# First norm's squares added on GpSimd, one product with ones in the middle of the second unit, and an output projection that waits tile by tile

## Chip, cores and metric

The kernel runs on one core of one Trainium2 chip. The metric is the device time of one execution in microseconds (us), lower is better; several executions are summed up by their median. In the text PE is the TensorE matrix engine, DVE the VectorE, ACT the ScalarE, POOL the GpSimd and SP the SyncE (it issues DMAs only).

## The reference

One decoder layer for 576 tokens (512 of a prompt, 64 of eight decode sequences), width 1024, feed-forward width 2816, all in float32:

```python
def rmsnorm(x, g):
    y = xf * lax.rsqrt(jnp.mean(xf * xf, axis=-1, keepdims=True) + RMS_EPS)
    return (y * g).astype(x.dtype)

def half_swiglu(x, g, w_gate, w_up, w_down):
    h = rmsnorm(x, g)
    return x + 0.5 * ((jax.nn.silu(h @ w_gate) * (h @ w_up)) @ w_down)

x = half_swiglu(x, ffn1...)                       # first feed-forward half step
proj = rmsnorm(x, mix_norm) @ w_in                # attention q/k/v, RWKV rows, gates
o_attn = ...dilated window attention...           # three groups of heads
o_rwkv = ...RWKV-7 time mixing...
merged = sigmoid(g_attn) * (o_attn @ w_branch_attn) + sigmoid(g_rwkv) * (o_rwkv @ w_branch_rwkv)
x = x + merged @ w_out                            # output projection
x = half_swiglu(x, ffn2...)                       # second feed-forward half step
```

Outputs are the new x, the key and value caches, the RWKV state and the token-shift rows.

## The kernel before

**Layout.** Everything is kept transposed: a tensor of width 1024 is 8 tiles (KD = 8) of 128 partitions by 576 tokens. A matmul covers 288 tokens, so each tile takes two.

**Three passes.** Float32 accuracy is had from splits: an operand is its high part (written by ACT as fp32r) plus its low part (value minus high part, by DVE for activations, by POOL for weights). One *slice* (`unit_slice`, L343) is the six matmuls of one input tile: high by high, low by high, high by low, twice 288 columns. One *unit* is the slices that make one tile of 128 output columns: 8 slices for weights of 1024 rows (`W8`, 128x1024 elements). Units come in pairs P with two sides q = 0 and 1, each side with its own `w_raw`, `w_hi`, `w_lo` and PSUM banks (side 0 writes banks 0 and 1, side 1 banks 2 and 3, banks 4 and 5 take the norm's sums). There are 101 pairs.

**The flow of a unit's weights.** SP loads `w_raw` (L319) once POOL has finished the pair before; ACT copies it to `w_hi` (`split_hi`, L325) once PE has finished with the old one; POOL subtracts to `w_lo` (`split_lo`, L330); PE waits for that (`unit_wait`) and for its PSUM banks to be read.

**The first norm.** `first_act` and `first_dve` go over the 8 tiles of x. DVE multiplies a tile by the gain (`h_gained`, L464), ACT copies the product to `h_hi` (`h_high`, L455), DVE subtracts to `h_lo` (`h_low`, L460). ACT also squares each tile (`square`, L421) into one of two buffers, and PE adds the squares over partitions by a float32 product with a matrix of ones (`sum_squares`, L428), one product for each of the 8 tiles, each put ahead of that tile's slice of the very first unit. A third square waits until PE has read the first one. The weights are split after the second and the fourth tile. After the last product the root follows: Ln and Exp on ACT (L367, L368), a refinement on DVE (L375, L376, L379) that ends in `nry`. DVE multiplies `nry` into the first unit's result (L596), ACT applies Silu to it (L560), and only after that, in ACT's own order, splits the weights of the next pair.

**The middle and the second norm.** The norm ahead of w_in and the one ahead of the second feed-forward step add their squares on DVE (`add_square`, L402) and need one product with ones (`sum_all`, L408).

**Merge and output projection.** `merge_pe` runs four units of the attention branch in halves, whose results DVE reads from PSUM bank pairs, multiplies by a gate (L2131) and adds to the RWKV half (L2135). ACT writes `m_hi` (L2108), DVE `m_lo` (L2121), which counts `m_ready` up by one for each of the 8 merged tiles, from 1. The output projection is pairs P_OUT to P_OUT+3; PE starts it when `m_ready` is 8, that is with seven tiles, and waits for the eighth before its slice. DVE adds each unit to x (L2144).

Every engine runs its instructions in the written order, and waits only on semaphores.

## Time and profile before

| | |
|---|---|
| median of 3 runs | 1896.87 us |
| lowest, highest | 1893.55, 1899.52 us |
| the profiled execution | 1897.97 us |
| its span, first to last instruction | 1896.1 us |
| PE busy | 1791.2 us, 94% of the span |
| DVE, ACT, POOL busy | 41%, 32%, 28% |
| mean granted TensorE clock | 0.973 of full |

The profile is one execution recorded by the hardware. Its rows give a start and a length in us from the span's start; the bracket behind a row is how long the engine had been idle and what ended the wait. A clock of 1.00 is 2.4 GHz and 0.50 is 1.2 GHz. Times below are span times; the execution's own time is 1.9 us more than its span.

### The profile page before, as it was taken

The page shows a single profiled execution, that of the slowest core. Times are in us where ns is not written, and L with a number is a line of the kernel's source. Part 1 is how long each engine was busy: PE and PEld are TensorE (multiplying, and loading weights), DVE is VectorE, ACT ScalarE, POOL GpSimd, SP SyncE. Part 2 cuts the span into 40 slices and gives each one's busy share as a digit, 9 for nine tenths or more (in the row PEclk, how much of TensorE's full clock was granted, in tenths as well). Part 3 has the DMA queues.
Part 4 walks back from the last instruction along what each step waited for, and adds up shares of the span by engine and source line. Part 5 has one row for each costly group of instructions (what it writes and reads, how often), then busy time and mean ns, then how long its engine had stood idle before and what let it go on. Part 6 is the DMA issues. An engine that isn't in the chain of part 4 may idle for free.

```text
span 1896.1 us, 41228 instructions
## 1 busy us (share of the span) xinstructions
PE 1791.2 (94%) x17032; PEld 1700.9 (90%) x17032; DVE 769.4 (41%) x1111; ACT 610.0 (32%) x806; POOL 537.3 (28%) x210
## 2 busy tenths in 40 slices
PE   6999999997989898989979999999989999999999
PEld 6999999996989898988758989898889999999999
DVE  4333023323564545552367272727367333113320
ACT  4332122222524242422134253435223333123321
POOL 2333333332312121211012222223223343433432
PEclk9999999998999999999789999999989999999999
DMA  4333233331533232321034444535443333334343
GB/s 159 111 122 130 103 111 129 130 123 51 187 127 105 79 134 106 112 70 48 34 126 167 160 161 145 194 131 188 167 188 127 106 112 132 127 100 133 111 142 123
DMA packets 53111, 237.49 MB, mean 125 GB/s; under 512 B 7040, under 2 KB 7680, under 8 KB 51584
## 3 DMA queue, kind: packets, MB, share of 16 engines
q1 hardware_dynamic: 45120, 219.40, 33.6%
q10 hardware_dynamic: 7872, 16.37, 2.3%
q8 instruction: 91, 1.49, 0.3%
q14 instruction: 28, 0.23, 0.0%
HBM read 217.98 MB, written 71.76 MB: 153 GB/s over the span
## 4 chain that ended last, share of the span: by engine, by line
PE 55%; issue 24%; DVE 11%; POOL 5%; ACT 2%; DVEq 1%; ACTq 1%; POOLq 0%; PEldq 0%; PEld 0%
PE ps L343 41%; POOL w_lo L330 5%; PE ps L785 3%; DVE qkv L1932 2%; DVE work L375 1%; DVE work L376 1%; PE ps L1791 1%; DVE qkv L1089 1%; PE ps L1729 1%; DVEq L1983 1%; PE ps L1715 1%; ACT w_hi L325 1%; DVE probs L379 0%; DVE xx L1130 0%; PE ps L1329 0%
## 5 line engine op out<-in xcount | busy, mean ns | idle before, releaser
L330 POOL TENSOR_TENSOR w_lo<-w_raw,w_hi 128x1024 fp32r<-128x1024 f32 (+1 forms) x202 | 531.5, 2631 | 1339.6 <-ACT w_hi L325 1339.6
L343 PE MATMUL ps<-h_hi,w_hi 128*128 128x288 f32 x2464 | 556.1, 308 | 23.9 <-DVE h_lo L460 10.7
L343 PE MATMUL ps<-h_lo,w_hi 128*128 128x288 f32 x2464 | 531.3, 298 | 0.0
L343 PE MATMUL ps<-h_hi,w_lo 128*128 128x288 f32 x2464 | 531.2, 297 | 0.0
L343 PEld LDWEIGHTS ps<-h_hi,w_hi 128*128 128x128 f32 x2464 | 401.6, 191 | 48.8 <-issue 19.7
L343 PEld LDWEIGHTS ps<-h_lo,w_hi 128*128 128x128 f32 x2464 | 401.4, 191 | 0.0
L343 PEld LDWEIGHTS ps<-h_hi,w_lo 128*128 128x128 f32 x2464 | 400.8, 191 | 0.0
L325 ACT ACTIVATE w_hi<-w_raw 128x1024 fp32r<-128x1024 f32 (+1 forms) x204 | 226.3, 1109 | 460.2 <-PE ps L343 442.9
L343 PE MATMUL ps<-g_hi,w_hi 128*128 128x288 f32 x704 | 151.4, 297 | 0.1
L343 PE MATMUL ps<-g_lo,w_hi 128*128 128x288 f32 x704 | 151.2, 296 | 0.0
L343 PE MATMUL ps<-g_hi,w_lo 128*128 128x288 f32 x704 | 151.0, 296 | 0.0
L599 DVE SCALAR_TENSOR_TENSOR gt<-ps,nry 128x576 f32<-128x576 f32 x44 | 33.4, 758 | 241.3 <-PE ps L343 241.3
L612 DVE SCALAR_TENSOR_TENSOR x<-ps,x 128x576 f32 (+1 forms) x32 | 24.2, 758 | 236.0 <-PE ps L343 236.0
L343 PEld LDWEIGHTS ps<-g_hi,w_hi 128*128 128x128 f32 x704 | 113.6, 188 | 1.1 <-POOL w_lo L330 1.1
L343 PEld LDWEIGHTS ps<-g_lo,w_hi 128*128 128x128 f32 x704 | 113.7, 189 | 0.0
L343 PEld LDWEIGHTS ps<-g_hi,w_lo 128*128 128x128 f32 x704 | 113.7, 188 | 0.0
L605 DVE TENSOR_TENSOR g_lo<-gt,g_hi 128x576 f32 x44 | 87.6, 1990 | 42.2 <-ACT g_hi L565 42.2
L560 ACT ACTIVATE sg<-sg 128x576 f32<-128x576 f32 x44 | 30.2, 687 | 161.0 <-DVE sg L596 161.0
L596 DVE SCALAR_TENSOR_TENSOR sg<-ps,nry 128x576 f32<-128x576 f32 x44 | 33.4, 758 | 91.1 <-PE ps L343 90.6
L1352 ACT ACTIVATE qkv<-ps 128x576 f32<-128x576 f32 x36 | 23.4, 651 | 137.8 <-PE ps L343 137.7
L1013 ACT ACTIVATE zz<-ps 128x256 f32<-128x256 f32 x40 | 15.4, 384 | 90.5 <-PE ps L785 89.3
L560 ACT ACT_TABLE_LOAD x30 | 38.5, 1283 | 13.2 <-issue 13.2
(369 smaller groups left out, 1962.5 us busy)
## 6 DMA issues: line engine op xcount, KB each, us to landing
w_raw<-in_w SPq DMA_DIRECT2D x172, 512.0 KB, 3.7
w_raw<-in_w SPq DMA_DIRECT2D x32, 704.0 KB, 4.0
kv<-in_kc SPq DMA_DIRECT2D x32, 576.0 KB, 6.5
kv<-in_vc SPq DMA_DIRECT2D x32, 576.0 KB, 7.7
cache_out<-in_cache SPq DMA_DIRECT2D x28, 576.0 KB
gates<-gate_out ACTq DMA_DIRECT2D x16, 288.0 KB, 2.3
cache_out<-in_cache SPq DMA_DIRECT2D x8, 480.0 KB
kvT<-qkv ACTq DMA_DIRECT2D x4, 864.0 KB, 7.8
```

The source lines that it names most:

```text
L325: nc.scalar.activation(w_hi[par_][:, 0:words], w_raw[par_][:, 0:words], ACT.Copy).then_inc(hi_done, 1)
L330: nc.gpsimd.tensor_tensor(w_lo[par_][:, 0:words], w_raw[par_][:, 0:words], w_hi[par_][:, 0:words].bitcast(F32), ALU.subtract).then_inc(lo_ ...
L343: last = nc.tensor.matmul(ps[:, b + c, 0:HC], w[par_][:, wk], a[:, k, c * HC:(c + 1) * HC], start=(first and k == 0), stop=(end and k == n ...
L375: own(nc.vector.tensor_tensor(rt, ry, ry, ALU.mult))
L560: nc.scalar.activation(sg[:, :], sg[:, :], ACT.Silu).then_inc(sem("silu_done"), 1)
L596: nc.vector.scalar_tensor_tensor(two(sg[:, :]), bank2(0), back(0), two(nry[:, :]), ALU.mult, ALU.mult).then_inc(evac[0], 1)
L599: nc.vector.scalar_tensor_tensor(two(gt[:, :]), bank2(2), back(0), two(nry[:, :]), ALU.mult, ALU.mult).then_inc(evac[1], 1)
L605: nc.vector.tensor_tensor(g_lo[:, j, :], gt[:, :], g_hi[:, j, :].bitcast(F32), ALU.subtract).then_inc(sem("g_ready"), 1)
L612: nc.vector.scalar_tensor_tensor(two(x[:, k, :]), bank2(2 * q), 0.5, two(x[:, k, :]), ALU.mult, ALU.add)\
L785: last = nc.tensor.matmul(ps[rows_of(e), 4 + (2 * n + h) % 4, 64 * T:64 * T + 64], lhs(T, e), rhs(T, e), start=True, stop=True)
L1352: nc.scalar.activation(two(QKV[:, g, kind, :]), bank2(bank), ACT.Copy).then_inc(evac[q], 1)
L1932: V.scalar_tensor_tensor(a, a, P1("qg" if kind == 0 else "kg", g), ary[i % 2], ALU.mult, ALU.mult)\
```

## The change

Four edits at the start of the kernel and one at the output projection:

- The first norm's squares are added up in `nrt_first` by POOL (`add_first`), seven additions of 128x576: three after the split of the first weights, four after the split of the second. ACT writes the first square straight into `nrt_first`; its square k from k = 3 on waits for addition k-2.
- PE makes one product with ones, `sum_all(pe, 0)`, between slices 3 and 4 of the second unit, in place of eight in the first unit.
- ACT splits the first weights after the first square, ahead of the first `h_high` (before: after the second tile).
- The parameters follow the first two tiles of x in ACT's DMA queue; the first part of the constants goes behind all of x. ACT's first square now waits for the parameters too.
- The first unit pair of the output projection is written out of its loop: unit 0 waits for merged tile k ahead of slice k.

```diff
-        ACC = (None, nrt_first, mA)
+        ACC = (nrt_first, nrt_first, mA)
...
-            pe.wait_ge(sem("sq_added"), 7 * m)
+            pe.wait_ge(sem("sq_added"), 7 * m + 7)
...
-            if m:
-                if k == 0:
-                    out = ACC[m]
-                elif k >= 3:
-                    act.wait_ge(sem("sq_added"), 7 * (m - 1) + k - 2)
-            elif k >= 2:
-                act.wait_ge(sem("sq_summed"), k - 1)
+            if k == 0:
+                out = ACC[m]
+            elif k >= 3:
+                act.wait_ge(sem("sq_added"), 7 * m + k - 2)
...
                 if k % 2 == 0:
-                    act.wait_ge(sem("x_loaded%d" % (k // 2)), 16)
+                    act.wait_ge(sem("x_loaded%d" % (k // 2)), 16 if k else 32)
                 square(act, 0, k, k % 2)
+                if k == 0:
+                    split_hi(act, 0, 0, W8)
                 h_high(act, 0, k, k % 2)
-                if k in (1, 3):
-                    split_hi(act, 0, k // 2, W8)
+                if k == 3:
+                    split_hi(act, 0, 1, W8)
...
-            if f == 0:
-                pe.wait_ge(sem("con_loaded"), 32)
-                sum_squares(pe, 0, 0, 0, start=True)
             unit_wait(pe, P0, 0)
             for k in range(KD):
-                if f == 0 and k:
-                    sum_squares(pe, 0, k, k % 2, stop=(k == KD - 1))
...
-            unit(pe, P0, 1)
+            unit_wait(pe, P0, 1)
+            for k in range(KD):
+                if f == 0 and k == KD // 2:
+                    pe.wait_ge(sem("con_loaded"), 16)
+                    sum_all(pe, 0)
+                last = unit_slice(1, h_hi, h_lo, k, k, KD, 2)
+            last.then_inc(unit_done, 1)
...
+        def add_first(pool, k):
+            pool.wait_ge(sem("sq_ready"), k + 1)
+            nc.gpsimd.tensor_tensor(ACC[0][:, :], ACC[0][:, :], SQ[0][k % 2][:, :], ALU.add).then_inc(sem("sq_added"), 1)
+            pool.drain()
...
+            split_lo(pool, P0, 0, W8)
+            if P0 == P_FFN1:
+                for k in range(1, 4):
+                    add_first(pool, k)
+            split_lo(pool, P0, 1, W8)
+            if P0 == P_FFN1:
+                for k in range(4, KD):
+                    add_first(pool, k)
...
-            pe.wait_ge(sem("m_ready"), KD)
-            units_and_squares(pe, 2, P_OUT, lambda P, q: unit(pe, P, q, m_hi, m_lo, ready=("m_ready", 1, KD - 1)))
+            unit(pe, P_OUT, 0, m_hi, m_lo, ready=("m_ready", 1, 0))
+            unit(pe, P_OUT, 1, m_hi, m_lo)
+            with pe.Fori(1, 4) as j:
+                for q in range(2):
+                    unit(pe, P_OUT + j, q, m_hi, m_lo)
...
-                    act.dma_start(con[:, 0:CFIRST], t["con"][:, 0:CFIRST]).then_inc(sem("con_loaded"), 16)
-                    act.dma_start(par[:, :, 0], t["par"]).then_inc(sem("con_loaded"), 16)
+                    act.dma_start(par[:, :, 0], t["par"]).then_inc(sem("x_loaded0"), 16)
+            act.dma_start(con[:, 0:CFIRST], t["con"][:, 0:CFIRST]).then_inc(sem("con_loaded"), 16)
```

How this moves instructions. ACT at the start, before (rows of the program's order: line, operation, output from inputs, size, what it waits for):

```order
L421 ACTIVATE sq<-x 128x576 [waits x_loaded0]
L455 ACTIVATE h_hi<-hf_first 128x576 [waits hf_ready]
L421 ACTIVATE sq<-x 128x576
L455 ACTIVATE h_hi<-hf_first 128x576 [waits hf_ready]
L325 ACTIVATE w_hi<-w_raw 128x1024 [waits w_loaded_even]
L421 ACTIVATE sq<-x 128x576 [waits sq_summed,x_loaded1]
```

and after (lines have shifted; L418 is the square, L444 the high part):

```order
L418 ACTIVATE nrt_first<-x 128x576 [waits x_loaded0]
L325 ACTIVATE w_hi<-w_raw 128x1024 [waits w_loaded_even]
L444 ACTIVATE h_hi<-hf_first 128x576 [waits hf_ready]
L418 ACTIVATE sq<-x 128x576
L444 ACTIVATE h_hi<-hf_first 128x576 [waits hf_ready]
L418 ACTIVATE sq<-x 128x576 [waits x_loaded1]
```

The split of the first weights stands one square and two high parts earlier, and the third square waits for PE no more.

POOL at the start has nothing but the two splits before; after, with the additions as L632:

```order
L330 TENSOR_TENSOR w_lo<-w_raw,w_hi 128x1024 [waits hi_done]
L632 TENSOR_TENSOR nrt_first<-nrt_first,sq 128x576 [waits sq_ready] x3
L330 TENSOR_TENSOR w_lo<-w_raw,w_hi 128x1024 [waits hi_done]
L632 TENSOR_TENSOR nrt_first<-nrt_first,sq 128x576 [waits sq_ready] x4
L637 UNCONDITIONAL_BRANCH
```

So POOL has nine instructions in the stretch in which DVE makes `h_lo`, where it had two.

PE in the middle of the second unit, after; before, these slices followed each other with no product between:

```order
L343 MATMUL ps<-h_hi,w_hi 128x288 x2
L343 MATMUL ps<-h_lo,w_hi 128x288 x2
L343 MATMUL ps<-h_hi,w_lo 128x288 x2
L408 MATMUL ps<-nrt_first,con 128x288 [waits sq_added,con_loaded]
L408 MATMUL ps<-nrt_first,con 128x288
L343 MATMUL ps<-h_hi,w_hi 128x288 x2
L343 MATMUL ps<-h_lo,w_hi 128x288 x2
```

Twelve slices stand ahead of the one product with ones; seven stood ahead of the last of the eight.

## Rows read from the trace of the kernel before

**Rows 1.** The page: busy time of each engine, share of the span, instructions

```profile
PE 1791.2 (94%) x17032; PEld 1700.9 (90%) x17032; DVE 769.4 (41%) x1111; ACT 610.0 (32%) x806; POOL 537.3 (28%) x210
```

**Rows 2.** DMAs: size, issue to landing; timeline of the first rows: start, length, instruction

```profile
con<-in_con ACTq DMA_DIRECT2D x1, 192.0 KB, 6.4
...
1.25 0.45 ACTq L2194 DMA_DIRECT2D con<-in_con  x1
...
6.66 0.68 ACT L421 ACTIVATE sq<-x 128x576 f32<-128x576 f32 x1 [0.65 <-DMA x<-in_xT]
8.85 1.14 DVE L464 TENSOR_SCALAR hf_first<-x,par 128x576 f32<-128x576 f32 x2 [8.85 <-DMA par<-in_par]
```

**Rows 3.** Timeline: first weights' split, first slice, ACT's longest wait, two later matmul pairs

```profile
11.70 1.06 ACT L325 ACTIVATE w_hi<-w_raw 128x1024 fp32r<-128x1024 f32 x1
12.83 2.40 POOL L330 TENSOR_TENSOR w_lo<-w_raw,w_hi 128x1024 fp32r<-128x1024 f32 x1 [12.38 <-ACT w_hi L325]
15.28 0.85 PE L343 MATMUL ps<-h_hi,w_hi 128*128 128x288 f32 x2 [4.13 <-POOL w_lo L330]
19.04 0.68 ACT L421 ACTIVATE sq<-x 128x576 f32<-128x576 f32 x1 [4.70 <-PE ps L428]
19.29 0.68 PE L343 MATMUL ps<-h_lo,w_hi 128*128 128x288 f32 x2
21.48 0.42 PE L343 MATMUL ps<-h_lo,w_hi 128*128 128x288 f32 x2
```

**Rows 4.** Timeline: last low part, last product, next pair, and the units behind it

```profile
28.37 0.76 DVE L460 TENSOR_TENSOR h_lo<-hf_first,h_hi 128x576 fp32r<-128x576 f32 x1 [0.68 <-ACT h_hi L455]
29.25 1.13 PE L428 MATMUL ps<-sq,con 128*128 128x288 f32 x4
37.49 5.20 POOL L330 TENSOR_TENSOR w_lo<-w_raw,w_hi 128x1024 fp32r<-128x1024 f32 x2 [13.34 <-ACT w_hi L325]
38.52 1.93 DVE L602 TENSOR_TENSOR gt<-sg,gt 128x576 f32<-128x576 f32 x1 [0.16 <-issue]
39.89 0.53 PE L343 MATMUL ps<-h_hi,w_hi 128*128 128x288 f32 x2 [2.32 <-POOL w_lo L330]
48.09 0.76 DVE L596 SCALAR_TENSOR_TENSOR sg<-ps,nry 128x576 f32<-128x576 f32 x1 [4.79 <-PE ps L343]
60.89 0.76 DVE L596 SCALAR_TENSOR_TENSOR sg<-ps,nry 128x576 f32<-128x576 f32 x1 [1.85 <-PE ps L343]
```

**Rows 5.** One POOL and one DVE instruction in the middle; the line's x4: shortest, median, longest ns

```profile
506.95 2.54 POOL L330 TENSOR_TENSOR w_lo<-w_raw,w_hi 128x1024 fp32r<-128x1024 f32 x1 [3.87 <-ACT w_hi L325]
...
507.33 2.48 DVE L1077 TENSOR_SCALAR qkv<-u_k,par 128x576 f32<-128x576 f32 x1
...
L1077 DVE TENSOR_SCALAR qkv<-u_k,par x4: 520/522/2483, 507.3 to 784.7; 128x576 f32<-128x576 f32 x4
L2250 POOL TENSOR_TENSOR rw_lo<-o_rw,rw_hi x4: 1421/1440/1457, 1319.5 to 1323.6; 128x576 fp32r<-128x576 f32 x4
```

**Rows 6.** Timeline of the merge: DVE's low parts, POOL's split, the output projection's first units

```profile
1404.33 0.76 DVE L2121 TENSOR_TENSOR m_lo<-sig_r,m_hi 128x576 fp32r<-128x576 f32 x1
...
1406.95 2.72 DVE L2121 TENSOR_TENSOR m_lo<-mrg,m_hi 128x576 fp32r<-128x576 f32 x1
1409.77 0.76 DVE L2121 TENSOR_TENSOR m_lo<-sig_r,m_hi 128x576 fp32r<-128x576 f32 x1
1418.06 0.76 DVE L2144 TENSOR_TENSOR x<-x,ps 128x576 f32<-128x576 f32 x1 [7.53 <-PE ps L343]
...
1406.23 2.83 POOL L330 TENSOR_TENSOR w_lo<-w_raw,w_hi 128x1024 fp32r<-128x1024 f32 x1 [5.20 <-ACT w_hi L325]
...
1410.07 0.82 PE L343 MATMUL ps<-m_hi,w_hi 128*128 128x288 f32 x2 [7.80 <-DVE m_lo L2121]
```

**Rows 7.** Stretches: length, busy time of each engine, PEclk the granted clock, DMA

```profile
1410.00:1412.80 2.80, 2.73 (x11) 2.77 (x12) 0.52 (x1) 0.00 (x0) 0.00 (x0) 0.50 1.01 375
...
40.70:43.90 3.20, 3.20 (x15) 3.20 (x15) 1.88 (x1) 1.85 (x2) 1.99 (x1) 0.50 0.59 173
```

More of the change, by code:

```diff
@@ L413, in square @@
             out = SQ[m][q]
-            if m:
-                if k == 0:
-                    out = ACC[m]
-                elif k >= 3:
-                    act.wait_ge(sem("sq_added"), 7 * (m - 1) + k - 2)
-            elif k >= 2:
-                act.wait_ge(sem("sq_summed"), k - 1)
+            if k == 0:
+                out = ACC[m]
+            elif k >= 3:
+                act.wait_ge(sem("sq_added"), 7 * m + k - 2)
             nc.scalar.activation(out[:, :], x[:, k, :], ACT.Square).then_inc(sem("sq_ready"), 1)
             act.drain()
-        def sum_squares(pe, m, k, q, start=False, stop=False):
-            pe.wait_ge(sem("sq_ready"), 8 * m + k + 1)
-            for c in range(2):
-                last = nc.tensor.matmul(ps[:, 4 + c, 0:HC], K("ones"), SQ[m][q][:, c * HC:(c + 1) * HC], start=start, stop=stop)
-            last.then_inc(sem("sq_summed"), 1)
         def units_and_squares(pe, m, P0, one):
@@ L435, in units_and_squares @@
                 one(P0 + j, 1)
-            if m == 1:
-                sum_all(pe, 1)
+            sum_all(pe, m)
         def splits_and_squares(act, m, P0, words):
@@ L637, in ffn_dve, with up, down @@
                     added(P0 + 15 + HALF + k // 2, k, k % 2, last=True)
+        def add_first(pool, k):
+            pool.wait_ge(sem("sq_ready"), k + 1)
+            nc.gpsimd.tensor_tensor(ACC[0][:, :], ACC[0][:, :], SQ[0][k % 2][:, :], ALU.add).then_inc(sem("sq_added"), 1)
+            pool.drain()
         def ffn_pool(pool, P0):
-            with pool.Fori(0, 2) as half:
-                with pool.Fori(0, HALF) as j:
+            def up(half, j0):
+                with pool.Fori(j0, HALF) as j:
                     for q in range(2):
                         split_lo(pool, P0 + 15 * half + j, q, W8)
+            def down(half):
                 with pool.Fori(0, 4) as j:
```

7 lines of the change are left out of this document (5 added, 2 removed).

## The prediction

> **What bounds the kernel now.** I read the page's busy times first: PE works 94% of the span [rows 1], and no other engine half of it. So the time is PE's work plus the places where PE stands still or runs at the low clock, and a change that takes little work from PE can gain only there. The timeline then gives the two places that this change touches. At the start PE idles until the first weights are split, works through the first unit with a product with ones ahead of each slice, and after the second unit waits again until 39.89 for the next pair's low weights [rows 3, 4]. From there on PE doesn't stop: two units take 60.89 - 48.09 = 12.80 us [rows 4], so one takes 6.40 and a slice 0.80. So the start is worth exactly what moves the 39.89. At the merge PE idles 7.80 us until the seventh merged tile is there [rows 6]. Between the two places the change touches nothing but code layout, so both shifts are carried to the end.
>
> **The start: what sets 39.89.** It is not PE's own work. The last product with ones ends at 29.25 + 1.13 = 30.38, and 9.51 us after that the next pair's first matmul starts [rows 4]; in between stand the root, multiplication into the first result, Silu, split, low part, each behind the one before. This chain is unchanged. The question is when the (now single) product ends.
>
> **Start, step 1: earlier weights.** The constants landed 1.25 + 6.4 = 7.65, the parameters at 8.85 [rows 2]. Without the constants ahead, the parameters come between 6.6 (the first x was used at 6.66) and 8.85; I take 7.8, which is 1.2 us behind their forerunner, as in the trace. The square then ends at 8.5, the split (1.06) at 9.7, POOL's low part (2.40) at 12.1, where it ended at 15.23 before [rows 3]. That is 3.1 us earlier. ACT's waits for PE vanish too, 4.70 us the longest [rows 3], and PE's eight products (1.13 each, [rows 4]) become one. But by step 2 DVE now sets the pace of this unit, so what both leave free goes into waiting for DVE.
>
> **Start, step 2: POOL and DVE block each other.** This is what the addition on POOL costs. While POOL subtracts, a DVE instruction on two SBUF tiles does not run: `m_lo` came at 1406.95, inside POOL's 1406.23 to 1409.06, and ended 0.61 after POOL (2.72 in place of 0.76) [rows 6]. A multiplication by a column, the form of `h_gained`, waits too: at 507.33, inside POOL's 506.95 to 509.49, it took 2.48 in place of 0.52, and ended 0.32 after POOL [rows 5]. The other way round, two low parts of 2.40 in a row took 5.20 with a DVE instruction between them, and the second ended 2.24 after that DVE instruction [rows 4]: POOL gets on about 0.15 before DVE's recorded end, and the two take turns. An addition is not in the trace; the nearest row is POOL's subtraction of the same size, 1.44 [rows 5], which I take (1.35 to 1.7 for the range, since a drain follows each).
>
> Here the Trainium skill speaks against this change: "SBUF — State Buffer", section "Who interferes with whom", says that GpSimd and a VectorE instruction with two SBUF inputs or in a 2-port mode lock each other out for a whole instruction, and that one with a single SBUF input outside these modes doesn't. Read so that `h_gained` (one input tile) is free, the sum would be that of the first rival below; the 2.48 us row says that it isn't.
>
> Nine POOL instructions (two splits, seven additions) now stand among DVE's sixteen. Stepping them through with these numbers, ACT at 0.69 for a square or high part: low part 0 comes at 10.5 in POOL's split and ends at 12.7 (first slice 12.8, before 15.28 [rows 3]); addition 1 to 14.0, `h_gained` 2 held to 14.3; addition 2 to 15.6, low part 1 held to 16.2; addition 3 to 17.5, `h_gained` 3 to 17.8; low parts 2 and 3 free, 18.7 and 20.1; split 1 to 22.4, `h_gained` 5 held to 22.7; addition 4 to 23.9, low part 4 to 24.6; addition 5 to 25.8, `h_gained` 6 to 26.1; addition 6 to 27.4, low part 5 to 28.1; addition 7 to 29.3, `h_gained` 7 to 29.6; low parts 6 and 7 at 30.5 and 31.3. Before, the last low part ended at 29.13 [rows 4]. So the 3.1 us of step 1 are gone before the last tile, and 2.2 more.
>
> **Start, step 3: the product stands later.** It waits for twelve slices in PE's order. Slices 6 and 7 of the first unit start at 30.5 and after it, then come four of the second unit, then the product (1.13, [rows 4]). A slice is 0.80 at 2.4 GHz and 1.44 at 1.2 GHz (six times 288 columns). PE stands still between slices up to then (eight slices over 19 us), so I take it to be at the low clock at 30.5. In two places where it went on without a stop it was at 0.50 for 2.8 and 3.2 us [rows 7]; in the first unit of the program it was still slow 4.0 us after its start at 15.28 (0.68 for two matmuls at 19.29) and fast at 21.48 (0.42), so after 4.7 to 6.2 us [rows 3]. I take 4.2 us, the middle: slices 6 and 7 end at 33.4, the next at 34.8, three fast ones at 37.2, the product at 38.3. All fast would be 36.5, all slow 41.1.
>
> **Start, sum.** 38.3 + 9.5 = 47.8 for the next pair's first matmul, against 39.89: **8.0 us later** (all fast 6.1, 6.2 us slow 8.8, all slow 10.7). The second unit is done by 42, so it is not late, and PE idles some 6 us in place of 2.3. Leaving PE at the low clock afterwards is paid in both: 39.89 to 48.05 is 8.16 for a unit of 6.40 [rows 4].
>
> **The output projection.** PE ended the attention branch at 1410.07 - 7.80 = 1402.27 [rows 6]. Merged tiles 5, 6 and 7 are ready at 1405.09, 1409.67 and 1410.53 [rows 6], the ones before earlier. The first unit's low weights were done by 1406.23 - 5.20 = 1401.03, when POOL fell idle [rows 6], and DVE had read its banks, which the tiles before 6 came from. So slices 0 to 5 run at once (6 x 0.80, to 1407.1, tile 5 in time), slice 6 from 1409.7, slice 7 from 1410.6 to 1411.4. Before, the first unit ended at 1418.0, when DVE read it [rows 6]: 6.6 us earlier. The next side's weights are ready at 1406.23 + 2.83 = 1409.06 [rows 6], in time. Against it stands the clock. Before, the 7.80 us cost 2.8 us at 0.50 after the restart [rows 7], within the 7.95 us of the first unit. Now PE idles 2.6 us; after 2.32 us of idleness at 39.89 the clock also fell, for 3.2 us [rows 4, 7]. So I take it to fall again: 1.6 us, as 3.2 us at half rate. The gain is **5.0 us** (4.6 to 6.9: a longer low stretch, or none and 0.3 us of the loop's entry saved, since 1410.07 is 0.4 after tile 6). DVE's own chain of the merge doesn't change, and the chain behind the projection moves with PE's units. The loop entered one pair later, and POOL's and PE's longer code, have no row; I take 0, with 0.5 either way.
>
> **Sum.** 8.0 - 5.0 = +3.0 us: span 1899.1, execution 1897.97 + 3.0 = 1901.0. The profiled execution is 1.1 above the median of the runs, so the median becomes 1896.87 + 3.0 = **1899.9 us**, 0.16% more. A measurement of this kernel can tell about 0.3%, 5.7 us, from no change: under 1891.2 is faster, over 1902.6 slower. Each part is larger than the difference.
>
> **Rivals.**
> - *DVE isn't held where it matters* (0.17). If `h_gained` ran beside POOL, the same stepping ends the last low part at 27.0 and, with PE's clock as above, starts the next pair at about 43.5; with nothing held, it ends at 24.2 (POOL's additions at 24.8), the product at 29.4 to 31.3, and the next pair starts at 38.9 to 40.8. So the start costs -1.0 to 3.6 and the projection gains 5.0: -6.0 to -1.4 together, median 1890.9 to 1895.5. For it: low parts 2 and 3 are free in my own stepping, so a shift in phase frees more. Against: no row of POOL at work shows such a DVE instruction at its normal length.
> - *PE stays at the low clock until the product* (0.15). This is the slower side: six slices and the product take the all-slow price, 41.1 + 9.5 = 50.6, 10.7 us late; less 5.0 that is +5.7, or 1902.6, and with the 4.6 or additions of 1.7 us it is 1904 to 1905. It decides from where the clock comes back 8 us or more after slice 6; the long slow stretch of the first unit before, 4.7 us or more, speaks for it [rows 3], the two stretches of 2.8 and 3.2 against [rows 7].
> - *The first unit isn't the brake at all* (0.06): POOL and DVE interleave and the clock is up early, so that the product ends near 29; the start gains 1, the projection 6.6, together 1889. The two rows of held DVE instructions speak against it.
> - *The tile-by-tile waits don't start the projection early* (0.05), because its weights or banks come late: the gain of 5 goes, and the median is 1904.9. The 1401.03 speaks against it.
> - The forecast has the remaining 0.57.
>
> **How the numbers follow.** The forecast's own range is 1897 to 1903: start 6.1 to 9.5, projection 4.6 to 6.9, and runs of the same kernel spread by 3 us either way. The range over the cases is 1891.5 to 1904.5: it takes in most of the first two rivals and leaves about 0.1 out on each side. Faster by over 0.3%: 0.12 (the third rival, and a third of the first with the runs' spread). Slower: 0.20 (the second rival mostly, the fourth, the tail of the forecast). Within: 0.68.
>
> **What would show it.** In the changed kernel's timeline: the first slice near 12.8; POOL's additions at about 1.45 alone and 1.9 when they follow a held DVE instruction; `h_gained` and low parts at 1.5 to 2.5 in place of 0.52 and 0.76; the last low part near 31; the product ending near 38 and the first matmul of the next pair near 48. In the merge: six slices right behind the attention branch, a gap of 2.6, the first unit read 6 to 7 us earlier after its own shift, a low clock behind the gap. Wrong would be: DVE instructions at normal length inside POOL's additions, a product before 34, or a projection that starts no earlier.

## The result

The changed kernel takes 1904.18 us (median of 13 executions, 1899.02 to 1914.7), the kernel before 1898.02 us (13 executions beside it): ratio 1.004, 95% interval 1.0026 to 1.0054. So it is slower by some 6 to 8 us. The prediction set 0.3% as what can be told; the middle of the interval lies above that, its lower end just below. The forecast was +3.0 us. Three further groups of executions of the changed kernel gave 1.0052, 1.0047 and 1.0046.

The page of the changed kernel's profile (1906.01 us, span 1904.2) gives PE the same busy time as [rows 1] within 1 us, and 7 us more for DVE and 12 for POOL. The second row is one of its DMA queues: packets, MB, share of the 16 engines. 1.51 MB in 92 packets is 16.4 KB each (16,384 bytes in the trace). The profile calls this queue "instruction"; I read its packets as pages of the engines' code, which matter below.

```profile
PE 1792.1 (94%) x17004; PEld 1703.0 (89%) x17004; DVE 776.3 (41%) x1111; ACT 610.1 (32%) x806; POOL 549.5 (29%) x217
...
q8 instruction: 92, 1.51, 0.3%
```

**The start** in the changed kernel's timeline (start, length, engine, line, instruction, idle time ahead and what ended it). It answers to [rows 2 to 4]; L343 and L330 keep their lines, `h_gained` is now L453, `h_low` L449, the addition L632, the product L408.

```profile
7.54 0.68 ACT L418 ACTIVATE nrt_first<-x 128x576 f32<-128x576 f32 x1 [1.90 <-DMA par<-in_par]
...
9.45 2.35 POOL L330 TENSOR_TENSOR w_lo<-w_raw,w_hi 128x1024 fp32r<-128x1024 f32 x1 [9.00 <-ACT w_hi L325]
...
11.76 1.93 POOL L632 TENSOR_TENSOR nrt_first<-nrt_first,sq 128x576 f32<-128x576 f32 x1
12.50 1.49 DVE L453 TENSOR_SCALAR hf_first<-x,par 128x576 f32<-128x576 f32 x1
...
12.55 0.82 PE L343 MATMUL ps<-h_hi,w_hi 128*128 128x288 f32 x2 [12.55 <-DVE h_lo L449]
...
13.84 1.42 POOL L632 TENSOR_TENSOR nrt_first<-nrt_first,sq 128x576 f32<-128x576 f32 x1 [0.16 <-issue]
...
19.88 2.46 DVE L453 TENSOR_SCALAR hf_first<-x,par 128x576 f32<-128x576 f32 x1
...
29.37 1.61 DVE L449 TENSOR_TENSOR h_lo<-hf_first,h_hi 128x576 fp32r<-128x576 f32 x2
...
37.35 1.13 PE L408 MATMUL ps<-nrt_first,con 128*128 128x288 f32 x4
...
47.98 0.85 PE L343 MATMUL ps<-h_hi,w_hi 128*128 128x288 f32 x2 [6.31 <-POOL w_lo L330]
```

Everything is where the prediction put it, and the next pair starts 8.1 us later than the 39.89 of [rows 4].

**The merge** of the changed kernel, which answers to [rows 6, 7]; the last row is a stretch (length, busy time of PE, PEld, DVE, ACT, POOL, granted clock, DMA share, GB/s).

```profile
1417.24 0.43 PE L343 MATMUL ps<-m_hi,w_hi 128*128 128x288 f32 x2
...
1424.53 0.84 PE L343 MATMUL ps<-m_hi,w_hi 128*128 128x288 f32 x2 [2.33 <-DVE m_lo L2135]
...
1427.88 0.76 DVE L2158 TENSOR_TENSOR x<-x,ps 128x576 f32<-128x576 f32 x1 [2.55 <-PE ps L343]
...
1424.50:1427.90 3.40, 3.37 (x14) 3.37 (x15) 0.78 (x2) 0.03 (x1) 0.00 (x0) 0.51 0.91 308
```

PE had ended the attention branch at 1417.40. The projection's first matmuls stand right behind it, PE waits 2.33 us for the seventh tile, and runs at half the clock (0.51, the level of 1.2 GHz) behind it. The first result is read at 1427.88 against 1418.06: 9.8 us later, where PE ended the attention branch 15.1 us later (1417.40 against 1402.27). So the projection gave back 5.3 us there.

It gave back 1.5 us more further on. In the kernel before, PE waits 2.33 us at 1480.40 for the first weights of the second feed-forward step and falls to the low clock; in the changed kernel it waits as long and doesn't (first two rows before, then two after, then the two stretches of 4.20 us behind the wait):

```profile
1480.40 0.53 PE L343 MATMUL ps<-h_hi,w_hi 128*128 128x288 f32 x2 [2.33 <-POOL w_lo L330]
...
1481.89 0.69 PE L343 MATMUL ps<-h_lo,w_hi 128*128 128x288 f32 x2
...
1490.36 0.53 PE L343 MATMUL ps<-h_hi,w_hi 128*128 128x288 f32 x2 [2.33 <-POOL w_lo L330]
...
1491.52 0.42 PE L343 MATMUL ps<-h_lo,w_hi 128*128 128x288 f32 x2
...
1480.40:1484.60 4.20, 4.20 (x20) 4.20 (x21) 2.44 (x2) 1.97 (x2) 2.80 (x1) 0.59 0.48 141
...
1490.36:1494.56 4.20, 4.20 (x31) 4.20 (x32) 2.47 (x2) 1.97 (x2) 2.82 (x1) 1.00 0.47 139
```

This isn't the chance of one profile: of the 12 profiles below with the projection by tiles 11 have no low clock there (after_r3 has), and all 8 without it have. No run shows why. So from the end of the attention branch to 1500 us the edit of the projection is worth 6.3 to 6.8 us in those 11.

**What was not forecast** lies between. I matched PE's instructions one by one in both traces. The stretch from 440.10 to 1400.10 of the kernel before holds no edited line, and the same 10,349 matmuls take 6.6 us longer in the changed kernel. First the kernel before, then the changed one (same columns as above):

```profile
440.10:1400.10 960.00, 885.72 (x10349) 800.85 (x10348) 491.63 (x836) 330.40 (x512) 191.31 (x79) 0.95 0.36 130
```

```profile
448.65:1415.24 966.59, 890.60 (x10350) 805.70 (x10349) 492.12 (x837) 331.07 (x513) 191.21 (x79) 0.95 0.36 129
```

PE is busy for 4.9 us more with the same work, which is the low clock, and stands still for 1.7 us more (966.59 - 890.60 = 75.99 against 74.28). The bill of the two profiles: start +8.1, up to 440 us +0.5, the untouched stretch +6.6, projection -5.3, behind it -1.8 (the 1.5 of the low clock that is missing at 1481 us, and 0.3 in small pieces), together +8.1, as the spans say. The question for the experiments is the 6.6.

### The profile page after: what moved, and what is told of

Same layout as the page of the kernel before. It is cut to its first block, busy times and chain, and to the rows that moved or that the text cites. A ratio compares the mean times of both kernels' runs of the same rounds, so it can differ in the third digit from the quotient of the medians.

```text
span 1904.2 us, 41116 instructions
## 1 busy us (share of the span) xinstructions
PE 1792.1 (94%) x17004; PEld 1703.0 (89%) x17004; DVE 776.3 (41%) x1111; ACT 610.1 (32%) x806; POOL 549.5 (29%) x217
## 3 DMA queue, kind: packets, MB, share of 16 engines
q8 instruction: 92, 1.51, 0.3%
## 4 chain that ended last, share of the span: by engine, by line
PE 60%; issue 17%; DVE 13%; POOL 4%; ACT 3%; DVEq 1%; ACTq 1%; POOLq 1%; DMA 0%; PEldq 0%; PEld 0%
PE ps L343 45%; POOL w_lo L330 4%; PE ps L796 3%; DVE qkv L1943 2%; PE ps L1802 1%; DVE work L375 1%; DVE work L376 1%; PE ps L1740 1%; DVE m_lo L2135 1%; PE ps L1726 1%; ACT w_hi L325 1%; DVE qkv L1100 1%; PE ps L1746 1%; DVEq L1994 1%; PE ps L1710 1%
## 5 line engine op out<-in xcount | busy, mean ns | idle before, releaser
L330 POOL TENSOR_TENSOR w_lo<-w_raw,w_hi 128x1024 fp32r<-128x1024 f32 (+1 forms) x202 | 532.5, 2636 | 1334.8 <-ACT w_hi L325 1334.7
L343 PE MATMUL ps<-h_hi,w_hi 128*128 128x288 f32 x2464 | 558.3, 309 | 44.0 <-DVE h_lo L449 30.9
L343 PE MATMUL ps<-h_lo,w_hi 128*128 128x288 f32 x2464 | 534.0, 299 | 0.0
L343 PE MATMUL ps<-h_hi,w_lo 128*128 128x288 f32 x2464 | 533.4, 298 | 0.0
L343 PEld LDWEIGHTS ps<-h_hi,w_hi 128*128 128x128 f32 x2464 | 403.0, 192 | 68.7 <-POOL w_lo L330 23.5
L343 PEld LDWEIGHTS ps<-h_lo,w_hi 128*128 128x128 f32 x2464 | 404.1, 192 | 0.0
L343 PEld LDWEIGHTS ps<-h_hi,w_lo 128*128 128x128 f32 x2464 | 403.1, 192 | 0.0
L343 PE MATMUL ps<-g_hi,w_hi 128*128 128x288 f32 x704 | 151.5, 297 | 0.1
L343 PE MATMUL ps<-g_lo,w_hi 128*128 128x288 f32 x704 | 151.1, 296 | 0.0
L343 PE MATMUL ps<-g_hi,w_lo 128*128 128x288 f32 x704 | 151.0, 296 | 0.0
L343 PEld LDWEIGHTS ps<-g_hi,w_hi 128*128 128x128 f32 x704 | 113.6, 188 | 1.1 <-POOL w_lo L330 1.1
L343 PEld LDWEIGHTS ps<-g_lo,w_hi 128*128 128x128 f32 x704 | 113.7, 188 | 0.0
L343 PEld LDWEIGHTS ps<-g_hi,w_lo 128*128 128x128 f32 x704 | 113.7, 188 | 0.0
```

What stands on the lines that cost most here:

```text
L330: nc.gpsimd.tensor_tensor(w_lo[par_][:, 0:words], w_raw[par_][:, 0:words], w_hi[par_][:, 0:words].bitcast(F32), ALU.subtract).then_inc(lo_ ...
L343: last = nc.tensor.matmul(ps[:, b + c, 0:HC], w[par_][:, wk], a[:, k, c * HC:(c + 1) * HC], start=(first and k == 0), stop=(end and k == n ...
```

## The experiments

### Each half alone: e_start and e_proj

e_start is the changed kernel with one wait ahead of the projection for all eight tiles (diff below, against the changed kernel); e_proj is the kernel before with the projection by tiles, the change's own edit of `merge_pe` and nothing else.

```diff
-            unit(pe, P_OUT, 0, m_hi, m_lo, ready=("m_ready", 1, 0))
-            unit(pe, P_OUT, 1, m_hi, m_lo)
-            with pe.Fori(1, 4) as j:
+            pe.wait_ge(sem("m_ready"), KD)
+            with pe.Fori(0, 4) as j:
                 for q in range(2):
-                    unit(pe, P_OUT + j, q, m_hi, m_lo)
+                    unit(pe, P_OUT + j, q, m_hi, m_lo, ready=("m_ready", 1, KD - 1))
```

> The kernel before with the edits at the start alone (squares added on GpSimd, one product with ones, first weights split first, DMA order); the output projection waits for seven merged tiles as before. Theory A (the start costs what the changed kernel's trace shows, 39.89 to 47.98, and the rest of the excess, some 7 us that came up between 461 and 922 us, is bound to the start's edits): next pair's first matmul at 48, median 8 plus 3 to 7 us above before, +11 to +15. Theory B (the middle's excess belongs to the projection's longer code): +8. Theory C (the middle drifts by chance from execution to execution): +8 in the median, with a wider spread of runs.

> The kernel before with the tile-by-tile output projection alone. The first unit of the projection ends about 6.6 us earlier and loses 1.6 us at the low clock: -5.0 us in the median under theories A and C. Theory B (the longer code costs time in the middle): -2 or more, with the excess between 461 and 922 us visible in its trace.

Measured (each ratio here and below is to executions of the kernel before that ran beside it): e_start 1913.48 us, ratio 1.0078 (1.0052 to 1.0104); its next pair starts at 48.36, +8.5, and the untouched stretch is 9.1 us longer. e_proj 1889.70 us, ratio 0.9961 (0.9941 to 0.998), untouched stretch +0.3. So the excess comes with the start's edits, and the projection by tiles is a gain that stands alone. In e_proj's profile it is 5.1 us at the first result and 6.6 with the low clock that is missing behind it. Its loop's other place and longer code cost nothing that can be seen.

### The price of the additions, and of a mere delay: e_tiny and e_late

e_tiny is the changed kernel with additions of 8 of the 576 columns; it leaves the rest of the first norm's sum out.

```diff
-            nc.gpsimd.tensor_tensor(ACC[0][:, :], ACC[0][:, :], SQ[0][k % 2][:, :], ALU.add).then_inc(sem("sq_added"), 1)
+            nc.gpsimd.tensor_tensor(ACC[0][:, 0:8], ACC[0][:, 0:8], SQ[0][k % 2][:, 0:8], ALU.add).then_inc(sem("sq_added"), 1)
```

e_late is the kernel before with eleven more squares on ACT behind the root, which only delays the first unit's evacuation.

```diff
             root_act(act, own, 0)
+            for _ in range(11):
+                nc.scalar.activation(SQ[0][0][:, :], x[:, 0, :], ACT.Square)
+                act.drain()
```

> The changed kernel with GpSimd's seven additions cut to 8 of 576 columns (this leaves most of the first norm's sum out), same waits and order. If the two engines' holding each other is what costs the start, the h_gained and low part instructions fall to 0.52 and 0.76 us wherever no weight split runs, the last low part ends at 24 to 25 in place of 31, and the next pair starts at 40 to 41.5 in place of 47.98: 6.5 to 8 us less than the changed kernel, 1896 to 1898. If instead the later place of the product in PE's order is the cost, it stays within 2 us of the changed kernel.

> The kernel before with eleven more Square activations (0.77 us each, results unused) on ScalarE behind the first norm's Exp, so that the first Silu and with it the next pair come some 8 us later; nothing else is changed, nothing runs on GpSimd. If a start that is 8 us late costs its 8 us and no more, +8 us in the median and the middle as before. If the phase in which the middle is entered matters (theory A, by the DMAs and the clock), the trace shows an excess of some us between 461 and 922 us and the median is +11 to +15.

In e_tiny's timeline DVE's multiplication is back at its own length beside the small additions, and still held for 2.46 us by POOL's split, which is full size; the next pair starts at 39.14, a little before the 40 to 41.5 expected.

```profile
12.76 0.52 DVE L453 TENSOR_SCALAR hf_first<-x,par 128x576 f32<-128x576 f32 x1
...
17.16 2.46 DVE L453 TENSOR_SCALAR hf_first<-x,par 128x576 f32<-128x576 f32 x1
...
12.88 0.45 POOL L632 TENSOR_TENSOR nrt_first<-nrt_first,sq 128x8 f32<-128x8 f32 x1 [0.16 <-ACT sq L418]
...
39.14 0.85 PE L343 MATMUL ps<-h_hi,w_hi 128*128 128x288 f32 x2 [6.32 <-POOL w_lo L330]
```

So the size of POOL's additions is worth 47.98 - 39.14 = 8.8 us at the start: steps 2 and 3 of the prediction hold by their cause too. But e_tiny takes 1896.02 us, ratio 0.9989 (0.997 to 1.0009), where +0 at the start and -5 to -6.8 at the projection should have given 1891 to 1893: its untouched stretch is 7.0 us longer, without any delay ahead of it. e_late is the counterpart: 1905.47 us, 1.0044 (1.0024 to 1.0063), the 7.7 us of its delay and nothing else, untouched stretch -0.4. A delay doesn't make the excess, and the excess doesn't need one.

### Theory A, PE's code pages: e_startpad, e_b200, e_pool, e_best

The products' removal leaves 14 matmuls fewer in PE's program ahead of everything else, which the trace shows as 28 matmul and 28 weight-load records. Theory A: every later PE instruction then lies at another place of its 16 KB code page, and PE stops where a page of code comes late. Empty instructions (drains) at the beginning put the places back or move them.

e_startpad is e_start with the lines below; e_b200 is the kernel before with the same lines and 200 in place of 56.

```diff
             begin(pe, "pe")
+            for _ in range(56):
+                pe.drain()
```

e_pool is the kernel before with POOL's feed-forward code written as in the changed kernel, without the additions. e_best is e_proj with the parameters ahead of the constants and the first weights split first, the products left on PE:

```diff
-                    act.dma_start(con[:, 0:CFIRST], t["con"][:, 0:CFIRST]).then_inc(sem("con_loaded"), 16)
-                    act.dma_start(par[:, :, 0], t["par"]).then_inc(sem("con_loaded"), 16)
+                    act.dma_start(par[:, :, 0], t["par"]).then_inc(sem("x_loaded0"), 16)
+                    act.dma_start(con[:, 0:CFIRST], t["con"][:, 0:CFIRST]).then_inc(sem("con_loaded"), 16)
...
+                if k == 0:
+                    split_hi(act, 0, 0, W8)
                 h_high(act, 0, k, k % 2)
-                if k in (1, 3):
-                    split_hi(act, 0, k // 2, W8)
+                if k == 3:
+                    split_hi(act, 0, 1, W8)
...
-            dve.wait_ge(sem("con_loaded"), 32)
...
-                pe.wait_ge(sem("con_loaded"), 32)
+                pe.wait_ge(sem("con_loaded"), 16)
```

> The start's edits alone, as in e_start (1913.5 us, 0.78% more than before), with 56 empty TensorE instructions (drains) at the beginning of PE's program, where PE waits for the first weights anyway. They put back the number of PE instructions that the start's edits take away (14 products with ones, 4 instructions each), so that every later PE instruction lies at the same place of its 16 KB code page as in the kernel before. Theory A, the drift of 7 to 10 us in the middle stage is PE's instruction fetch meeting other code positions: the start still costs 8 us, the drift in the middle (460 to 922 us) is under 1.5 us, about 1905.5 us, ratio 1.004. Theory B, the drift comes from POOL's code or from another phase of the whole machine: the 56 instructions change nothing, 1913 us, drift 7 to 10 us.

> The kernel before with 200 empty TensorE instructions (drains) at the beginning of PE's program and no other edit. 200 is 256 less 56: with 256 instructions of 64 B in a 16 KB page, PE's later code lies at the same place of its page as in the changed kernel. Theory A (PE's instruction fetch): a drift of some 7 us in the middle although neither the start nor POOL is changed, 1905 us if the drains end before the first weights at 15.3 us; if they take longer, what they take longer comes on top at the start and the drift stays. Theory B: no drift in the middle, 1898 us, or 1898 plus what the drains take beyond 15.3 us.

> The kernel before with POOL's feed-forward code written as in the changed kernel (the first pair's two splits ahead of the loop, the two halves unrolled), without the additions. PE's code is that of before. Theory A: as before, ratio 1.000, no drift in the middle. Rival (POOL's own code layout causes the drift): a drift of some 7 us in the middle, 1905 us.

> The kernel before with the projection tile by tile (as e_proj, 1889.7 us) and, of the start, only what gives time without GpSimd: the parameters loaded ahead of the constants, the first weights split behind the first square. The squares are still summed by TensorE's eight products, so PE has the same number of instructions ahead of the middle. By the start's rows the first slice comes at 12.8 to 13.5 in place of 15.3 and the last product 1.5 to 3 us earlier: next pair at 37 to 38.5 in place of 39.9, no drift in the middle (theory A), 1887 to 1888.5 us, ratio 0.995. If the first unit is paced by VectorE's chain alone, the start gives nothing: 1889.7 us.

| kernel | median us | ratio (95%) | next pair | untouched stretch |
|---|---|---|---|---|
| e_startpad | 1907.18 | 1.0050 (1.0031 to 1.0069) | +9.0 | +2.8 |
| e_b200 | 1903.93 | 1.0044 (1.0021 to 1.0068) | +2.3 | +3.0 |
| e_pool | 1897.18 | 0.9984 (0.9963 to 1.0005) | -0.2 | -0.6 |
| e_best | 1892.17 | 0.9971 (0.9954 to 0.9988) | -2.7 | +6.8 |

POOL's code is out. For the other three the answer was mixed: the times of e_startpad and e_b200 are near those of theory A (e_b200's drains also delay the next pair by 2.3 us, of which 0.8 is left at 440 us; e_startpad's stretch is 2.8 us longer, where under 1.5 was expected), but e_best, with PE's code in place, has the excess too. Its start gave 2.7 us (37.18 against 39.89), and it is no faster than e_proj. Two things came out when I compared where PE and DVE stand still.

First, **PE's stop moves with the code.** In the small matmuls of L796 (L785 of the kernel before) e_tiny stops behind 32 and 20 of them, for nothing that the profile shows:

```profile
545.33 1.15 PE L796 MATMUL ps<-xt,lmask 64*64 64x64 f32 x32
546.49 0.80 PE L796 MATMUL ps<-xx,zz 64*64 64x64 f32 x20
548.74 0.56 PE L796 MATMUL ps<-xx,zz 64*64 64x64 f32 x12 [1.44 <-issue]
```

A kernel with PE's code put back (e_afterall2, below) stops 27 recorded matmuls earlier in the same run of them:

```profile
552.94 0.97 PE L796 MATMUL ps<-xt,lmask 64*64 64x64 f32 x25
555.85 0.39 PE L796 MATMUL ps<-xt,lmask 64*64 64x64 f32 x6 [1.95 <-issue]
```

In the trace of the kernel before, which stops at neither, the two places lie 27 matmuls, 27 weight loads and two semaphore waits (L780) apart. That is 56 instructions, the very number that the change removed. Over all profiles the later place stopped PE by 1.40, 0.62 and 2.27 us in three of four executions of the changed kernel, by 1.44, 0.35 and 0.35 in e_tiny, e_b200 and e_afterda; the earlier one by 1.80, 1.40, 0.41 and 1.95 in e_best, e_afterpad, e_afterall and e_afterall2, and not in the rest. No kernel stops at the other's place. A second place, L894 (L883 before), stops PE in all eight profiles with moved PE code (0.56 to 1.99 us) and in none of the other twelve; the changed kernel's:

```profile
864.79 0.37 PE L894 MATMUL ps<-tok 64*64 64x64 f32 x8 [0.89 <-issue]
```

The trace also shows what PE stopped for. Each of these 18 stops (10 at the two places of the small matmuls, 8 at L894) ends 1.32 to 1.62 us after a packet of 16,384 bytes of the instruction queue has landed. In e_tiny the packet takes from 546.30 to 547.18, PE runs out at 547.3 and goes on at 548.74; in after_r3 it takes from 554.90 to 555.78, and PE goes on at 557.25. In the kernel before the packet had landed at 543.90, some 2.2 us before PE came to the earlier place. So PE waits for code that comes late; why it is asked for late in one execution and not in another, no run shows.

The Trainium skill, "Runtime: NRT & Kernel Launch", section "Instruction fetch mechanics", says that an engine fetches its code in 16 KiB blocks of 256 instructions and that the cost is "mostly hidden". The place and the packets' size agree with that (200 more and 56 fewer give the same positions), the hiding doesn't: up to 2.27 us here, in code that the kernel writes out without a loop.

Second, **DVE's code is one instruction shorter** in the changed kernel and in e_best, e_start, e_startpad, e_tiny and e_afterpad (below), because the wait for `con_loaded` is gone. In all nine profiles of these DVE stops at L379 near 797 us and at L1166 near 567 us of the kernel before, 0.36 us more than the 0.09 between two instructions, and at L2057 near 1140 us (0.33 more); in none of the eleven with the full count. No packet of either instruction queue lands in the 2 us ahead of these stops, so a late page isn't what the traces show for DVE. What the stop at L379 does is plain in the changed kernel's timeline (DVE, then POOL, then PE):

```profile
806.83 0.76 DVE L379 SCALAR_TENSOR_TENSOR sw<-tmp,sw 128x576 f32<-128x576 f32 x1 [0.45 <-issue]
...
812.98 2.82 DVE L1105 TENSOR_TENSOR qkv<-u_k,exp_m 128x576 f32<-128x576 f32 x1
815.90 0.76 DVE L1107 TENSOR_TENSOR qkv<-u_r,exp_p 128x576 f32<-128x576 f32 x1
...
821.51 0.76 DVE L1116 TENSOR_TENSOR bonus<-ps,qkv 128x576 f32<-128x576 f32 x1 [2.37 <-PE ps L768]
...
812.83 2.37 POOL L330 TENSOR_TENSOR w_lo<-w_raw,w_hi 128x1024 fp32r<-128x1024 f32 x1 [2.19 <-ACT w_hi L325]
...
815.86 0.66 PE L761 MATMUL ps<-con,qkv 128*128 128x128 f32 x4 [1.47 <-DVE qkv L1105]
...
817.88 0.68 PE L343 MATMUL ps<-h_lo,w_hi 128*128 128x288 f32 x2
```

DVE comes to L1105 at 812.98, 0.15 us behind POOL's split, and is held for 2.82 us. PE waits 1.47 for it, falls to the low clock (0.68 for two matmuls that take 0.42), and DVE waits 2.37 us for its next input. With DVE's instruction given back (e_afterda, below) L1105 gets in first and the next one is held. PE waits 1.47 us for that one too, but only after four matmuls more, and runs on at full clock:

```profile
807.04 0.76 DVE L379 SCALAR_TENSOR_TENSOR sw<-tmp,sw 128x576 f32<-128x576 f32 x1
...
813.19 0.76 DVE L1105 TENSOR_TENSOR qkv<-u_k,exp_m 128x576 f32<-128x576 f32 x1
814.04 2.76 DVE L1107 TENSOR_TENSOR qkv<-u_r,exp_p 128x576 f32<-128x576 f32 x1
...
820.10 0.76 DVE L1116 TENSOR_TENSOR bonus<-ps,qkv 128x576 f32<-128x576 f32 x1 [0.81 <-PE ps L768]
```

This exchange of places stands in all nine profiles with DVE's code one instruction shorter and in none of the other eleven. In six of the nine PE falls to the low clock behind it and DVE is 1.6 us later at its next input; in e_start, e_startpad and e_best PE stays at full clock, and nothing is lost there.

### Is it the kernel, or one execution? after_r1, after_r2, before_r1, before_r2

Both kernels again, unedited. Theory C was that the low-clock stretches fall anew in every execution, and that the 6.6 us are one draw.

> The changed kernel again, unedited. Theory C: how much of the middle stage PE spends at the low clock, and so how long that stage takes, is drawn anew in every execution; the 7 us by which the middle stage (460 to 922 us of before) was longer in the profile of the changed kernel are one draw. Then a second and a third execution give another length, anywhere from 0 to 8 us over before's profile, with the low-clock time in step. Theory D (it belongs to the changed kernel): the same 7 us again, at the same places.

> The kernel before again, unedited. Theory C: in some of its own executions the middle stage is longer by 2 to 8 us than in its first profile, with low-clock stretches at other places, since its times spread from 1892.7 to 1911.2 us at mean granted clocks of 0.976 to 0.965. Theory D: the same middle as in its first profile within 1 us.

> As after_r1: the changed kernel again, unedited. Theory C: another length of the middle stage than in the other two executions (0 to 8 us over before's first profile). Theory D: the same 7 us at the same places.

> As before_r1: the kernel before again, unedited. Theory C: a middle stage that may differ by 2 to 8 us from its first profile. Theory D: within 1 us of it.

Medians 1906.86 and 1906.68 us against 1898.16 and 1899.12. The two repeats of the unedited kernel before had ratios of 1.0016 (0.9999 to 1.0034) and 1.0020 (1.0004 to 1.0035), so a ratio that is 0.002 off says little here. The untouched stretch is longer than in the first profile of before by 9.7 and 13.2 us (changed), by 0.1 and 2.1 us (before). So C is right in part: within one kernel the stretch varies by 2 to 7 us, and in before_r1 a shift of up to 5.2 us built up between 500 and 701 us and was down to 0.7 at 1223 us. But the changed kernel's stretch never came near that of before. The longest one (after_r2) in one row: 11.3 us more of PE's busy time at a clock of 0.94, and 1.9 us more of standing still.

```profile
448.02:1421.20 973.18, 896.98 (x10349) 807.35 (x10348) 492.11 (x837) 331.11 (x513) 191.28 (x79) 0.94 0.36 128
```

### Putting the code back: e_afterpad, e_afterall, e_afterda, after_r3, e_bestdve

The changed kernel with 56 drains on PE (e_afterpad), one on DVE and one on ACT, whose code is one instruction shorter too (e_afterda), or all of them (e_afterall, e_afterall2); and e_best with one drain on DVE alone.

```diff
 (e_afterall)
             begin(pe, "pe")
+            for _ in range(56):
+                pe.drain()
...
             begin(act, "act")
+            act.drain()
...
             begin(dve, "dve")
+            dve.drain()
```

> The changed kernel with 56 empty TensorE instructions (drains) at the beginning of PE's program, which put every later PE instruction back to its place in the 16 KB code pages. Theory A (code positions of PE): PE's stalls at L785 (0 to 1.4 us) and L883 (0.6 to 2.0 us) are gone and with them most of the low clock that follows; 1899 to 1902 us, 4 to 6 us below the changed kernel on the same chip. Theory B (the excess has nothing to do with PE's code): as the changed kernel, 1905 to 1907 us.

> As e_afterpad, and one drain at the beginning of VectorE's and of ScalarE's program, whose code is one instruction shorter in the changed kernel. Theory A with DVE's part: the two DVE stalls of 0.36 us (L1166, L379) and the exchange of places between L1094 and L1096 are gone too, the stages between 460 and 1000 us are as in the kernel before within 2 us, 1898 to 1901 us. If DVE's positions are worth nothing: as e_afterpad. Theory B: 1905 to 1907 us.

> The changed kernel again, unedited, on the chip of the two padded kernels. Theory A: 1904 to 1907 us, PE's stall at L883 of 0.5 to 2.0 us again. Theory B: the same time, as the two padded ones.

> e_best (1892.2 us) with one drain at the beginning of VectorE's program, so that all engines have their code at the positions of the kernel before. If DVE's one instruction less is what takes 5 us of e_best's gain: 1887 to 1888.5 us, no excess between 460 and 1000 us. If not: 1892 us.

> The changed kernel with one drain at the beginning of VectorE's and one of ScalarE's program, PE's code where the changed kernel has it. If their one instruction is the whole cause: as e_afterall, 1901 to 1902.5 us, with PE's stall at L883 still there (0.5 to 2 us). If PE's positions count as much: 1903 to 1905 us. If only all three together count, or the difference between e_afterpad and e_afterall was chance: 1905 to 1907 us.

> e_afterall again, unedited: 1900 to 1903 us if the code positions are the cause of the excess; 1905 to 1907 us if its first 1901.5 us was chance. PE's stall of up to 1.8 us, if any, 56 instructions ahead of that of the changed kernel in the lines of L785; none at L883.

| changed kernel with | median us | ratio to before (95%) |
|---|---|---|
| nothing (after_r3) | 1906.89 | 1.0046 (1.0028 to 1.0064) |
| PE's code put back (e_afterpad) | 1905.66 | 1.0040 (1.0026 to 1.0054) |
| DVE's and ACT's (e_afterda) | 1903.31 | 1.0022 (0.9997 to 1.0047) |
| all three (e_afterall) | 1901.51 | 1.0013 (0.9991 to 1.0035) |
| all three (e_afterall2) | 1899.63 | 1.0007 (0.9987 to 1.0027) |

One execution of after_r3 took 3405.27 us and one of e_afterda 2463.68 us; the table's medians leave these two out.

With drains alone, which do no work, the changed kernel is 5 to 8 us faster by the ratios (1.0013 and 1.0007 against 1.0040 to 1.0052 in its four groups) and lands near the forecast's 1.0016, with its next pair at 47.26 and 47.66 as without them. It also lands on the sum of the parts: +8.1 at the start and some -6.5 at the projection make about +1.6 us, and 1.0013 and 1.0007 are +2.5 and +1.3. PE's code alone missed its forecast of 1899 to 1902 us. The row of the untouched stretch in e_afterall has PE's busy time of the kernel before again:

```profile
447.54:1409.39 961.85, 885.78 (x10349) 800.13 (x10348) 491.71 (x836) 330.26 (x512) 191.26 (x79) 0.96 0.36 130
```

e_bestdve took 1889.30 us, ratio 0.9956 (0.9942 to 0.9969), stretch +3.6: the forecast of 1887 to 1888.5 was too bold, and its 2.9 us below e_best lie within the intervals, so it doesn't show DVE's share. It and e_proj are the fastest kernels here, both below the kernel before and the changed one.

All 20 profiles by their code's place, as us by which the untouched stretch is longer than in the first profile of before. A profiled execution can be far from its group's median (after_r2's is 5.3 us above, e_afterda's 2.0 below), so the last column takes off by how much it was above:

| PE's code | DVE's code | profiles | mean | mean after that |
|---|---|---|---|---|
| as before | as before | before 0, 0.1, 2.1; e_late -0.4; e_proj 0.3; e_pool -0.6; e_bestdve 3.6; e_afterall 1.8; e_afterall2 5.6 | 1.4 | 0.3 |
| moved | as before | e_b200 3.0; e_afterda 2.2 | 2.6 | 4.5 |
| as before | one less | e_startpad 2.8; e_afterpad 6.1; e_best 6.8 | 5.2 | 3.4 |
| moved | one less | changed 6.6, 9.7, 13.2, 9.1; e_tiny 7.0; e_start 9.1 | 9.1 | 6.7 |

The first and the last row stand clear of each other, and each shift alone lies between. Which of the two weighs more isn't shown: the two middle rows change places between the columns, with two and three profiles, and by the times putting back either one alone (e_afterpad, e_afterda) gained less than the intervals can tell.

## Why the prediction was wrong

The step that failed is the last sentence on the projection: "The loop entered one pair later, and POOL's and PE's longer code, have no row; I take 0, with 0.5 either way", together with "Between the two places the change touches nothing but code layout, so both shifts are carried to the end". I had seen the layout and priced it at nothing, and I looked at the code that grew, not at the 56 PE instructions and the one DVE instruction ahead of everything that vanished. The two together are worth 5 to 8 us in time, more than the whole forecast, and they pushed the result over the bound of 1902.6. A second term that was put at nothing is smaller and of the other sign: "the chain behind the projection moves with PE's units" left out the low clock at 1481 us, 1.5 us that the change saves. The other steps, in their order:

- **Step 1** held: parameters at 7.54 (7.8 forecast), low part at 11.80 (12.1), first slice at 12.55 (12.8).
- **Step 2** held: additions of 1.42 us alone and up to 1.93 behind a held DVE instruction (1.44 and 1.9 forecast), `h_gained` at 1.49 and 2.46 in place of 0.52, last low part at 30.98 (31.3). The prediction read the Trainium skill's rule ("SBUF — State Buffer", "Who interferes with whom") as one that would leave `h_gained` free. But that section frees an instruction with one SBUF input only outside the 2-port modes, and names `tensor_scalar` among the operations that can enter one and then contend. `h_gained` is a `tensor_scalar`, and the trace agrees with that reading: held in the rows, and e_tiny shows that the additions are what holds it.
- **Step 3** held: product to 38.48 (38.3), next pair at 47.98 (47.8), +8.1 (+8.0). PE's low clock there lasted from 30.18 to about 35.3, 5.1 us against the 4.2 taken.
- **Projection** held: -5.3 (-5.0), wait of 2.33 (2.6), low clock 3.4 us (3.2). e_proj alone gave more in time, 7.4 us (3.8 to 11.2 by its interval), which the 1.5 us at 1481 us helps to explain.
- **Rivals**: the first (DVE not held) and the third (first unit not the brake) fell with step 2, the second with a product at 37.35, the fourth with the first matmul at 1417.24. The slower side came by none of them. The median stands inside the range of 1891.5 to 1904.5 by 0.3 us, by luck; the chance of 0.68 for "within 0.3%" was too high, since no term carried the layout.

Open: in the changed kernel's four profiles PE stands still in the stretch 1.7 to 4.5 us longer, and is busy 4.6 to 11.3 us longer, which is the low clock. For the place at 813 us a chain from the one to the other is shown above, though in three of nine profiles the clock didn't fall behind it; for the rest it is only argued that a stop lets the clock fall. That putting PE's code back alone (e_afterpad) gained nothing measurable agrees with its stop having only moved (1.40 us at the earlier place), but 12 executions don't settle PE's own share; e_b200, where only PE's code is moved, has 1.0044. Why one instruction makes DVE stop 0.36 us was not tried apart from counting it, and ACT's instruction was never moved without DVE's in the changed kernel (in e_best only DVE's was missing, and in e_late ACT had 22 more without harm).

## What to carry to other kernels

An edit at the start of a long straight-line program moves the code of everything behind it, so count the instructions per engine that it adds or removes and leave some 0.3% of the time open for it (here it was a loss; whether it can be a gain wasn't tried). When a change costs what no edited line explains, pad each engine with empty instructions back to its old count before looking for a mechanism: it separates what the edit does from where it puts the code, though for 0.3% it takes more than one group of executions. And judge a kernel by several profiles: the same kernel's untouched stretch differed by up to 7 us between executions.

## What the runs showed of the hardware

- PE stands still for 0.35 to 2.3 us at fixed positions of its program, which move one for one with the number of instructions ahead; whether and how long it stops at such a place varies between executions (0 to 2.27 us at the same one). All 18 such stops end 1.32 to 1.62 us after a packet of 16,384 bytes of the instruction queue has landed.
- A DVE instruction count off by one made three stops of 0.33 to 0.36 us, and at one place that was enough to change who gets in first, POOL or DVE: 0.15 us behind POOL cost DVE 2.06 us (2.82 in place of 0.76), and in six of nine profiles PE its clock.
- Much of the difference between executions is the granted clock: in the same 10,349 matmuls PE was busy 884.4 to 897.0 us.
- After the same wait of 2.33 us PE's clock fell in one kernel (0.59 over the next 4.20 us) and stayed up in the other (1.00).
